# Expert results gathered before the last item ends, and the last item's rows scattered by a gate-scaled table product

## What is computed

```python
top_logit, top_idx = lax.top_k(logits, TOP_K)
gates = jax.nn.softmax(top_logit, axis=-1)
...
hid = jax.nn.silu(xb @ w_gate[e]) * (xb @ w_up[e])
return hid @ w_down[e]
...
y = jnp.zeros((T, D), hn.dtype).at[row_tok].add(
    (yb.astype(jnp.float32) * row_g[:, None]).astype(hn.dtype))
```

## Time and profile before

| | |
|---|---|
| median of 3 runs | 1415.06 us (1413.07 to 1415.53) |
| profiled execution, span | 1414.1 us from first to last instruction; the profile gives no other time for it |
| busy share of the span | TensorE 95%, VectorE 24%, ScalarE 18%, GpSimd 2% |
| the chain that ended last | TensorE 92% of the span, VectorE 4%, ScalarE 2%, DMA 1%, issue 1% |
| start of item 0, of item 7 (the last) | 489.3 us, 1281.4 us |
| last down product ends | 1394.2 us |
| bytes | 434 MB read, 12 MB written |

### The profile page before, as it was taken

One profiled execution on the slowest core, in us unless ns is written; L12 is line 12 of the kernel. 1 busy time (PEld: TensorE's weight loads), 2 busy tenths in 40 slices (PEclk: granted clock), 3 DMA queues, 4 the chain that ended last, 5 costly groups with the idle time before them and its releaser, 6 DMA issues.

```text
span 1414.1 us, 32772 instructions
## 1 busy us (share of the span) xinstructions
PE 1349.5 (95%) x14759; PEld 798.3 (56%) x14759; DVE 344.5 (24%) x485; ACT 260.5 (18%) x396; POOL 21.2 (2%) x27
## 2 busy tenths in 40 slices
PE   6998999999979699999999999999999999999994
PEld 6997899988757434534533543443453453453352
DVE  5864555545765401000000000000000100000001
ACT  5463544444632100000000000000000000000000
POOL 0001000000000100000000000000000000000001
PEclk9999999999989899999999999999999999999997
DMA  9962465554701896999999999999999999999994
GB/s 320 350 230 74 138 198 182 180 195 162 246 22 60 339 365 229 360 406 322 408 420 383 390 418 398 378 416 408 367 413 419 366 412 419 360 409 420 380 383 170
DMA packets 123701, 442.50 MB, mean 313 GB/s; under 512 B 9060, under 2 KB 50356, under 8 KB 107188
## 3 DMA queue, kind: packets, MB, share of 16 engines
q1 hardware_dynamic: 117600, 424.75, 79.3%
q10 hardware_dynamic: 4820, 11.53, 2.3%
q0 software_dynamic: 1152, 4.19, 0.8%
HBM read 434.12 MB, written 12.08 MB: 316 GB/s over the span
## 4 chain that ended last, share of the span: by engine, by line
PE 92%; DVE 4%; ACT 2%; DMA 1%; issue 1%; ACTq 0%; POOL 0%; POOLq 0%; DVEq 0%
PE bank L1607 41%; PE bank L1622 21%; PE bank L1253 8%; PE bank L1255 8%; PE bank L1254 8%; PE bank L1652 1%; PE bank L1502 1%; PE bank L1665 1%; PE bank L1597 1%; PE bank L1391 1%; PE bank L1458 1%; DVE w_lo L784 0%; PE bank L1589 0%; DMA raw<-slot_rows,slot 0%; ACT w_hi L526 0%
## 5 line engine op out<-in xcount | busy, mean ns | idle before, releaser
L1607 PE MATMUL bank<-raw,xT 128*32 128x512 f32 (+1 forms) x4608 | 440.8, 539 | 3.7 <-issue 3.0
L1607 PEld LDWEIGHTS bank<-raw,xT 128*32 128x32 f32 x4608 | 151.7, 110 | 282.1 <-issue 282.1
L1622 PE MATMUL bank<-dn,hidT 128*32 128x256 f32 x5376 | 296.5, 379 | 0.0
L1622 PEld LDWEIGHTS bank<-dn,hidT 128*32 128x32 f32 x5376 | 172.3, 110 | 116.1 <-issue 4.4
L784 DVE TENSOR_TENSOR w_lo<-raw,w_hi 128x2048 fp32r<-128x2048 f32 x62 | 141.8, 2291 | 117.7 <-ACT w_hi L526 117.6
L1228 DVE TENSOR_TENSOR e_hid<-e_silu,bank 128x512 f32<-128x512 f32 (+1 forms) x48 | 26.9, 616 | 530.4 <-PE bank L1607 530.4
L1607 PE MATMUL bank<-up_more,xT 128*32 128x384 f32 (+1 forms) x1536 | 150.3, 539 | 0.0
L1253 PE MATMUL bank<-ht_hi,w_hi 128*128 128x256 f32 x480 | 137.2, 286 | 4.2 <-DVE w_lo L857 2.7
L1255 PE MATMUL bank<-ht_hi,w_lo 128*128 128x256 f32 x480 | 136.8, 285 | 0.0
L1254 PE MATMUL bank<-ht_lo,w_hi 128*128 128x256 f32 x480 | 135.7, 283 | 0.0
L526 ACT ACTIVATE w_hi<-raw 128x2048 fp32r<-128x2048 f32 x62 | 118.1, 1912 | 61.6 <-PE bank L1255 61.6
(11 more groups left out here) (246 smaller groups left out, 828.5 us busy)
## 6 DMA issues: line engine op xcount, KB each, us to landing
dn<-in_moe_w_down SPq DMA_DIRECT2D x112, 1024.0 KB, 12.6
raw<-in_moe_w_gate SPq DMA_DIRECT2D x48, 1024.0 KB, 13.5
raw<-in_moe_w_up SPq DMA_DIRECT2D x48, 1024.0 KB, 12.6
raw<-in_moe_w_gate SPq DMA_DIRECT2D x48, 768.0 KB, 9.3
raw<-in_moe_w_up SPq DMA_DIRECT2D x48, 768.0 KB, 6.3
up_more<-in_moe_w_gate SPq DMA_DIRECT2D x16, 1024.0 KB, 21.8
up_more<-in_moe_w_up SPq DMA_DIRECT2D x16, 1024.0 KB, 12.4
raw<-in_hgrn_w_in SPq DMA_DIRECT2D x15, 1024.0 KB, 12.1
```

Source lines behind the costliest of these rows:

```text
L1607: ins = nc.tensor.matmul(out_banks[j][GTOK * c:GTOK * c + GTOK, 0:w], xT[:, kt, GTOK * g:GTOK * g + GTOK], chunk[:, w * b:w * b + w], star ...
L1622: ins = nc.tensor.matmul(banks[6 + j // 2][GTOK * c:GTOK * c + GTOK, 256 * (j % 2):256 * (j % 2) + 256], tok, dn[:, i % DN_RING, D * half ...
```

## The change

The rows of all items but the last are fetched during the last item, and GpSimd multiplies them by their gates and adds them to `h` there. It waits for the stores of all items but one (`items[17]`), then issues four indirect fetches into a tile of its own, `early`, which lies over `ht_hi` and `ht_lo` (free by then). A choice whose slot belongs to the last item is pointed at row 1407, which is zero, by VectorE before the loop. The rows of the last item aren't fetched back. Instead VectorE builds, before the loop, a table `end_sel` [token, slot of the last item] that holds the gate where the token has that slot, and zero elsewhere. After the loop TensorE transposes it, VectorE copies it out, and TensorE multiplies it by `yb`, four products with 512 columns each. VectorE adds each to `h`, and SP stores each quarter of the output. The last item's store of `yb` is still made, by ScalarE as before.

The diff, cut to what does this (declarations of the small tiles and semaphores are left out):

```diff
+        with ExitStack() as over:
+            early = sb(over, "early", [P, TT, 2, D])
         ht_hi = sb(ctx, "ht_hi", [P, KT, T], f32r)
...
-        back = [[raw[:, t, D * i:D * i + D] for i in range(2)] for t in range(TT)]
...
+        END_BANKS = [banks[1], banks[2], banks[5], banks[0]]
...
             for t in range(TT):
-                sp.wait_ge(combined, t + 1)
-                sp.dma_start(out[0][P * t:P * t + P, :], h[:, t, :]).then_inc(stored, 16)
-            sp.wait_ge(stored, 16 * TT)
+                for half in range(2):
+                    cut = slice(512 * half, 512 * half + 512)
+                    sp.wait_ge(combined, 2 * t + half + 1)
+                    sp.dma_start(out[0][P * t:P * t + P, cut], h[:, t, cut]).then_inc(stored, 16)
+            sp.wait_ge(stored, 16 * TT * 2)
...
             pool.wait_ge(routed, 1)
-            n_items = pool.value_load(items[0:1, 16:17], min_val=E, max_val=MAX_ITEMS)
-            pool.wait_ge(y_stored, n_items * 16)
+            n_before = pool.value_load(items[0:1, 17:18], min_val=E - 1, max_val=MAX_ITEMS - 1)
+            pool.wait_ge(early_ready, 1)
+            pool.wait_ge(y_stored, n_before * 16)
             pool.sem_inc(pool_pace, 1)
             for t in range(TT):
                 for i in range(2):
-                    at = bass.IndirectOffsetOnAxis(ap=slot[:, t, i:i + 1], axis=0)
-                    nc.gpsimd.indirect_dma_start(out=back[t][i], out_offset=None, in_=slot_rows, in_offset=at).then_inc(fetched[t][i], 16)
+                    at = bass.IndirectOffsetOnAxis(ap=early_slot[:, t, i:i + 1], axis=0)
+                    nc.gpsimd.indirect_dma_start(out=early[:, t, i, :], out_offset=None, in_=slot_rows, in_offset=at).then_inc(fetched[t][i], 16)
+            for i in range(2):
+                for t in range(TT):
+                    pool.wait_ge(fetched[t][i], 16)
+                    rows = early[:, t, i, :]
+                    then(nc.gpsimd.tensor_scalar(rows, rows, gate[:, t, i:i + 1], None, MUL))
+                    if i:
+                        pool.wait_ge(early_added, t + 1)
+                    nc.gpsimd.tensor_tensor(h[:, t, :], h[:, t, :], rows, ADD).then_inc(early_added, 1)
...
+            nc.vector.tensor_scalar(itf[0:1, 17:18], which[0:1, E:E + 1], float(E - 1), None, ADD)
...
-            nc.vector.tensor_copy(items[0:1, 0:17], itf[0:1, 0:17])
+            nc.vector.tensor_copy(items[0:1, 0:18], itf[0:1, 0:18])
...
+            then(nc.vector.tensor_scalar(end_base[:, :], which[:, E:E + 1], float(CAP), float(CAP * (E - 1)), MUL, ADD))
+            then(nc.vector.tensor_scalar(end_pos[:, :, :], pos[:, :, :], end_base[:, :], None, SUB))
+            nc.vector.tensor_scalar(in_end[:, :, :], end_pos[:, :, :], 0.0, None, ALU.is_ge)
+            then(nc.vector.tensor_scalar(away[:, :, :], pos[:, :, :], -1.0, float(ZERO_ROW), MUL, ADD))
+            then(nc.vector.tensor_tensor(away[:, :, :], away[:, :, :], in_end[:, :, :], MUL))
+            then(nc.vector.tensor_tensor(away[:, :, :], away[:, :, :], pos[:, :, :], ADD))
+            nc.vector.tensor_copy(early_slot[:, :, :], away[:, :, :]).then_inc(early_ready, 1)
             dve.wait_ge(routed, 1)
+            for t in range(TT):
+                for i in range(2):
+                    ins = nc.vector.tensor_scalar(end_sel[:, t, i, :], const[:, K_IOTA:K_IOTA + CAP], end_pos[:, t, i:i + 1],
+                                                  gate[:, t, i:i + 1], ALU.is_equal, MUL)
+            then(ins)
+            then(nc.vector.tensor_tensor(end_sel[:, :, 0, :], end_sel[:, :, 0, :], end_sel[:, :, 1, :], ADD))
...
-            for t in range(TT):
-                for i in range(2):
-                    dve.wait_ge(fetched[t][i], 16)
-                    if i:
-                        dve.wait_ge(half_added, t + 1)
-                    nc.vector.scalar_tensor_tensor(out=h[:, t, :], in0=back[t][i], scalar=gate[:, t, i:i + 1], in1=h[:, t, :],
-                                                   op0=MUL, op1=ADD).then_inc(combined if i else half_added, 1)
+            dve.wait_ge(end_turned, 1)
+            nc.vector.tensor_copy(end_selT[:, :], banks[0][0:CAP, 0:T]).then_inc(end_sel_ready, 1)
+            dve.wait_ge(early_added, 2 * TT)
+            for t in range(TT):
+                for half in range(2):
+                    part = h[:, t, 512 * half:512 * half + 512]
+                    dve.wait_ge(end_full, 2 * t + half + 1)
+                    nc.vector.tensor_tensor(part, part, END_BANKS[2 * t + half][:, :], ADD).then_inc(combined, 1)
...
+            for t in range(TT):
+                ins = nc.tensor.transpose(banks[0][0:CAP, P * t:P * t + P], end_sel[:, t, 0, :], ident)
+            ins.then_inc(end_turned, 1)
+            pe.wait_ge(end_sel_ready, 1)
+            pe.wait_ge(yb_ready, n_items * 2 + 1)
+            for t in range(TT):
+                for half in range(2):
+                    nc.tensor.matmul(END_BANKS[2 * t + half][:, :], end_selT[:, P * t:P * t + P], yb[:, 512 * half:512 * half + 512],
+                                     start=True, stop=True).then_inc(end_full, 1)
```

More of the change, by code:

```diff
@@ L44 @@
 ROWS = 1408
+ZERO_ROW = ROWS - 1
 K_ID, K_ANTI, K_TRI, K_STRICT, K_IOTA, K_HOT, K_MASK, K_END = 0, 128, 256, 640, 768, 896, 1280, 1664
@@ L153, in build_program @@
         items = sb(ctx, "items", [1, 32], i32)
+        end_base = sb(ctx, "end_base", [P, 1])
+        end_pos = sb(ctx, "end_pos", [P, TT, 2])
+        in_end = sb(ctx, "in_end", [P, TT, 2])
+        away = sb(ctx, "away", [P, TT, 2])
+        early_slot = sb(ctx, "early_slot", [P, TT, 2], u32)
         dense = ExitStack()
@@ L215, in build_program @@
         gate = sb(ctx, "gate", [P, TT, 2])
+        end_sel = sb(ctx, "end_sel", [P, TT, 2, CAP])
+        end_selT = sb(ctx, "end_selT", [CAP, T])
         s = ExitStack()
@@ L338, in build_program @@
         fetched = [[sem(f"fetched{t}{i}") for i in range(2)] for t in range(TT)]
-        half_added = sem("half_added")
+        early_ready = sem("early_ready")
+        early_added = sem("early_added")
+        end_turned = sem("end_turned")
+        end_sel_ready = sem("end_sel_ready")
+        end_full = sem("end_full")
         combined = sem("combined")
```

## The result

The changed kernel takes 1397.4 us (median; 1397.0 to 1400.0) against 1414.6 in the runs beside it, 0.988 of it with an interval of 0.987 to 0.990. That is 17.2 us less.

The account below looks back on a forecast made before the run. TensorE alone bounds the expert loop; behind it a chain of copies, store, fetches and additions does. Tail gain 11.0 minus weight waits 0.7 gives 10.3 us off 1415.06, so 1404.8 us, range 1402.8 to 1409.0.

Parts of the forecast that it names:

- These 18.5 us: Behind the loop, from the last yb copy's end at 1395.62 us to the span's end at 1414.1.
- the tail: Behind the loop: transposes and table copy hidden, four products 3.6 us, last store 3.1; end at 1403.1, 11.0 us saved.
- GpSimd is early enough: Last item: GpSimd's fetches, multiplications and additions are done at 1324 us, over 70 us before VectorE asks.
- D: Rival, tail: slow GpSimd multiplications make VectorE wait, past 1414.1 us from 23.5 us each; chance 0.02.
- E: Rival, tail: fetches start only behind the last store, GpSimd's 19 us stand in the tail, about 1425 us; chance 0.01.
- the weights: Last item: 2.10 MB of fetches delay weight loads, so TensorE waits 0.4 us at up chunks, 0.3 at down, together 0.7.
- catching up: Last item, 1322 to 1342 us: the DMA backlog is worked off at about 417 GB/s, making up 3.0 us.
- remaining lag: Weight delay left when the last item's down chunks begin: 5.0 - 0.4 - 3.0 = 1.6 us.
- lead of the second chunk: Last item's second down chunk lands at 1356.7 us and is used at 1358.0, a lead of 1.3 us.
- B: Rival, last item: weights hurt more, nothing made up, TensorE waits 3.7 to 5.1 us; 1407.8 to 1409.2; chance 0.17.
- C: Rival, behind the loop: TensorE's new steps dearer by 1.4 to 3.6 us, 1406.2 or 1408.4; chance 0.08.
- A: Rival, last item: fetches hidden altogether, only the tail counts, 1404.1 us, or 1403.5 with shorter last stores; chance 0.16.

Follow-up runs that it names:

- e1: Changed kernel with its five small tiles declared behind the dense tiles, so w_hi and the rest lie where they lay before; 1403.9 us, ratio 0.993.
- e2: Kernel before with one unused tile of 160 bytes a partition ahead of the dense tiles; 1404.7 us, ratio 0.994.
- e5: Changed kernel without the four early fetches and GpSimd's eight passes, addresses unchanged; 1394.2 us.
- e9: Changed kernel with 64 unused bytes between the dense tiles and the loop's, putting up_more and dn at multiples of 128; 1394.2 us, ratio 0.986.
- e7: Changed kernel with 64 unused bytes a partition ahead of the dense tiles, w_hi at a multiple of 128; 1399.6 us.
- e10: Changed kernel with 64 unused bytes ahead of early and ht_hi, moving ht_hi and ht_lo to 64 past a multiple of 128; 1396.0 us.
- e6: Changed kernel with three more fetches of 0.5 MB each behind the four, into free tiles that nothing reads; 1402.9 us.
- e4: Kernel before with an unused tile of 64 bytes ahead of the dense tiles, w_hi still 32 past a multiple of 64; 1409.1 us, ratio 0.996.
- e8: Changed kernel with 320 unused bytes a partition ahead of the dense tiles, w_hi at a multiple of 512; 1402.2 us.

## Why the prediction was wrong, step by step

- **Wrong: what is rebuilt.** "These 18.5 us are what the change rebuilds" left out the declarations. The diff's five small tiles were read as storage that costs nothing, and every term of the sum was taken from behind 1280 us. The step that failed is this implied zero for everything ahead of the loop. In its place stand 7.5 us in the profiles, and 6.5 between the medians of e1 and the changed kernel; e1 and e2 show that they come from where `w_hi` and its neighbours lie. Why the place counts stays open. No rival covered it, so the range had no room below 1402.8 for it.
- **Right: the tail.** Forecast 11.0. The profiles give 11.6, of which 0.6 is the first trace's own (four other kernels with the old tail have 19.1 to 19.3 us there for its 19.9): 10.8 to 11.0 against those. The transposes and the table's copy hid, the products took 0.93 us each, clock full. That the sum came out so close is partly luck: the old tail that it started from was 0.6 us long, and the last store, put at 3.1 us, took 2.4.
- **Right: GpSimd is early enough** (the prediction's D and E fall): done at 1315.5, for 1324 forecast, and 8.6 us of the difference are the earlier start of the last item. Multiplications cost 2.85 us rather than 2.33; earlier landings made up for it.
- **Half right: the weights.** Mechanism, lag and catching up as forecast, the cost undersized: 1.5 us (e5) for 0.7. Of the visible waits 0.2 fell on the up chunks (0.4 forecast) and 1.0 on the down chunks (0.3). The term that was too small is the wait at the down chunks. It was put at the remaining lag (1.6 us) minus the lead of the second chunk (1.3), and the chunk that came late was the first. The prediction's B was there in small; its C didn't happen. A, nothing to wait for, is what e9 shows, where `dn` lies at a multiple of 128.
- **The sum** for the change alone was 10.3 us; e1 measures 10.0, with 7 to 12 us inside its interval, so that the agreement to 0.3 us is more than the runs can confirm. The 1.0 us between the median and the profiled span, by which 1403.8 became 1404.8, was read from that one long execution: in the 22 others of before, each time is 1.9 us above its span in the median. It cancels in the difference.

## What to carry to other kernels

A tile declared in the middle shifts all behind it, and that alone can be worth as much as a change: before a difference is credited to an edit, pin the addresses (new tiles at the end, or a pad) or run the old kernel with the new layout. Where stationary loads are busy all the time, try several distances between stationary and moving tiles; here 64 and 96 bytes modulo 128 were faster than 0, and 32 the slowest. Place tiles that receive streams at multiples of 256 bytes, as `dn` lay in e7 to e10. Transfers moved under a loop at full DMA share are free only up to the thinnest lead of the loads; here the next 1.57 MB cost their bytes in full (e6).

## What the runs showed of the hardware

- TensorE's float32r products of 128 x 128 by 256 columns run at 120.0, 118.7, 117.8, 116.7 or 113.3 ns a record, depending on the distance between stationary and moving operand modulo 128 bytes, all at full clock. At a distance of 64 two rhythms are possible in one program (113.3 and 117.8). The times of such kernels spread over 3 to 7 us in four runs; whether by the rhythm isn't shown, since each has one profile and kernels at other distances spread by 1 to 6. Why, and what picks the rhythm, stays open; a distance was tried only for these tiles.
- Transfers of 4 KB rows into a tile at a multiple of 128 (and of 256) bytes moved 417 to 418 GB/s, elsewhere 408 to 409, at a share of 1.02 to 1.03.
- Expectations that failed: alignment to 64 bytes (e4), round addresses as the best (e7, e8).
